# Prompt attention two iterations deep, its second top-k moved, and the gate tiles redistributed, in a two-layer hybrid encoder step

## The reference, cut to what matters

```python
def token_mixing(h, pos, past, w_in, b_forget, w_branch, w_out):
    qkv_sb, qkv_fox, f_logit, qkv_dsa, q_idx, k_idx, w_idx, gate_logit = jnp.split(h @ w_in, offs, axis=-1)
    ...
    o_sb = stick_breaking_attention(q_sb, ks_sb, vs_sb, pos, k_pos)
    o_fox = forgetting_attention(q_fox, ks_fox, vs_fox, g_all[:, -t:], g_all, pos, k_pos)
    o_dsa = dsa_attention(q_dsa, ks_dsa, vs_dsa, q_idx, w_idx, ks_idx, pos, k_pos)
    y = jnp.stack([o.reshape(b, t, MIX_W) for o in (o_sb, o_fox, o_dsa)], axis=2)
    y = jnp.einsum('btnc,ncd->btnd', y, w_branch)
    gates = jax.nn.sigmoid(gate_logit.reshape(b, t, N_BRANCH, D_MODEL))
    merged = jnp.sum(gates * y, axis=2)
```

## Time and profile before

| | |
|---|---|
| median of 3 runs | 2898.83 us (2898.41 to 2899.73) |
| the profiled execution | 2894.99 us, span 2893.2 us |
| TensorE matmul busy | 2642.7 us, 91% of the span |
| VectorE, ScalarE busy | 663.9 us (23%), 514.9 us (18%) |
| DMA moved | 389.01 MB, mean 134 GB/s |
| granted TensorE clock, mean | 0.962 |

### The profile page before, as it was taken

How to read it: one execution, slowest core, us unless ns; L and a number is a source line. 1 busy time by engine, 2 the same in 40 slices (tenths; PEclk the granted TensorE clock), 3 DMA queues, 4 the chain that set the end, 5 groups by cost and what they waited for, 6 DMA issues and landing times.

```text
span 2893.2 us, 32024 instructions
## 1 busy us (share of the span) xinstructions
PE 2642.7 (91%) x12900; PEld 1597.7 (55%) x12900; DVE 663.9 (23%) x1452; ACT 514.9 (18%) x1010; POOL 0.2 (0%) x4
## 2 busy tenths in 40 slices
PE   5999998997798899999969999999878979899997
PEld 3666554555565555555546665555555655455554
DVE  2111002024475421110021110100254754211101
ACT  2000002013443311000110000110235332300001
POOL 0000000000000000000000000000000000000000
PEclk8999999998999899999989999999999999999998
DMA  8555332351168531323275543324403694223231
GB/s 301 175 174 192 121 101 66 109 150 57 62 207 265 180 117 58 116 87 100 85 267 185 193 165 109 104 70 116 141 33 121 189 285 147 88 88 107 87 100 62
DMA packets 315597, 389.01 MB, mean 134 GB/s; under 512 B 33566, under 2 KB 269850, under 8 KB 315491
## 3 DMA queue, kind: packets, MB, share of 16 engines
q1 hardware_dynamic: 308418, 378.65, 39.6%
q10 hardware_dynamic: 7072, 8.87, 0.9%
HBM read 377.85 MB, written 9.62 MB: 134 GB/s over the span
## 4 chain that ended last, share of the span: by engine, by line
PE 85%; DMA 4%; ACT 4%; DVE 3%; SPq 2%; issue 1%; ACTq 0%; DVEq 0%
PE PS L556 29%; PE PS L597 16%; PE PS L631 11%; PE PS L653 8%; PE PS L843 3%; PE PS L853 3%; PE PS L576 3%; PE PS L534 2%; PE PS L800 2%; PE PS L770 2%; DMA RING<-w_ada 1%; DMA QKT<-cache_dsa_k 1%; PE PS L711 1%; PE PS L522 1%; PE PS L810 1%
## 5 line engine op out<-in xcount | busy, mean ns | idle before, releaser
L556 PE MATMUL PS<-H,RING 128*128 128x384 f32 x2560 | 843.0, 491 | 20.4 <-ACT H L914 20.4
L556 PEld LDWEIGHTS PS<-H,RING 128*128 128x128 f32 x2560 | 488.5, 192 | 360.9 <-issue 33.4
L597 PE MATMUL PS<-BIG,RING 128*128 128x384 f32 x1408 | 458.5, 489 | 9.3 <-DVE BIG L1226 9.3
L597 PEld LDWEIGHTS PS<-BIG,RING 128*128 128x128 f32 x1408 | 269.3, 191 | 198.2 <-issue 14.8
L631 PE MATMUL PS<-RING,H 128*128 128x384 f32 (+1 forms) x960 | 309.2, 486 | 6.8 <-ACT H L914 6.8
L653 PE MATMUL PS<-H,RING 128*128 128x384 f32 x768 | 257.5, 492 | 0.0
L631 PEld LDWEIGHTS PS<-RING,H 128*128 128x128 f32 x960 | 184.0, 192 | 132.2 <-issue 10.4
L1225 DVE TENSOR_TENSOR QR<-PS,QR 128x384 f32<-128x384 f32 x88 | 49.0, 557 | 838.3 <-ACT QR L922 838.3
L922 ACT ACTIVATE QR<-PS 128x384 f32<-128x384 f32 x88 | 43.1, 490 | 908.4 <-PE PS L556 825.3
L653 PEld LDWEIGHTS PS<-H,RING 128*128 128x128 f32 x768 | 145.1, 192 | 97.4 <-issue 6.0
L1181 DVE TENSOR_TENSOR QR<-QR,MOD 128x128 f32<-128x128 f32 x48 | 14.0, 292 | 537.9 <-ACT QR L931 537.9
(11 more groups left out here) (186 smaller groups left out, 1746.5 us busy)
## 6 DMA issues: line engine op xcount, KB each, us to landing
RING<-ffn_w_in SPq DMA_DIRECT2D x88, 1024.0 KB, 7.0
RING<-w_in SPq DMA_DIRECT2D x68, 768.0 KB, 6.1
QR<-w_ada SPq DMA_DIRECT2D x48, 1024.0 KB, 7.1
RING<-w_ada SPq DMA_DIRECT2D x24, 1024.0 KB, 7.4
RING<-ffn_w_out SPq DMA_DIRECT2D x32, 768.0 KB, 4.6
RING<-ffn_w_out SPq DMA_DIRECT2D x32, 640.0 KB, 5.7
QKT<-cache_sb_k SPq DMA_DIRECT2D x16, 768.0 KB, 6.8
QR<-cache_sb_v SPq DMA_DIRECT2D x16, 768.0 KB, 4.5
```

Of the source, the lines that this page charges most:

```text
L556: mm = pe.matmul(PS[:, 2 * jj + part, 0:T], w[:, k, part * 256 + jj * P:part * 256 + (jj + 1) * P], H[:, k, :], start=(k == 0), stop=(k == ...
L597: mm = pe.matmul(PS[:, m, 0:T], w[:, k, m * P:(m + 1) * P], HID[:, half * (NFF // 2) + k, :], start=(half == 0 and k == 0), stop=(half == ...
```

## The change

- **Prompt attention two deep.** `ZP` gets two buffers of two halves each, the softmax statistics two sets. TensorE issues the scores of `it + 2` between the transposes and the values of `it`. VectorE's loop is cut into `biased` (scale, bias, mask), `maxima` and `probs`, and runs `biased(it + 1)`, `probs(it)`, `maxima(it + 1)`; ScalarE runs `exponentials(it + 1)` between the copies of `it` and its output copy. A new semaphore `z_taken` says that the scores' PSUM banks are read. Sigmoids, the SB product and the maxima are made in two halves of three heads.
- **Top-k moved.** The first half's eight rounds go in pairs ahead of the four sample heads' sums in the index stage, the second half's eight into the prompt iterations 0, 2 and 3 (2, 3 and 3 rounds). Both keep their work arrays in `RSTD` and `VAR`.
- **Gate tiles.** None stands between the samples' index heads. Tiles 6 and 7 come after the last one, 8 to 12 at the ends of prompt iterations 0 to 4, 13 to 23 in sample steps 0, 1, 2, 4, 6, 8, 10, 12, 14, 16 and 18. All of 6 to 12 use PSUM bank 4, all of the steps' bank 3.
- **Sample steps.** The samples' 17 top-k rounds go to steps 0 to 8 and 10 (2, 2, 2, 1, 2, 1, 2, 1, 2, 2). The last two gate weight units load after `load_step(2)` and `load_step(7)`; the mask is stored after `load_step(12)` instead of 10.

```diff
-GATES = [6, 8, 9]
-GATE_AT = [9, 10, 11, 12, 13, 14, 15]
-GATE_STEP = {s: GATE_AT[6] + s for s in range(9)}
-ROUND_STEP = {s: 2 for s in range(8)}
+GATES = 6
+GATE_PROMPT = [GATES + 1 + it for it in range(6)]
+GATE_STEP = dict(zip((0, 1, 2, 4, 6, 8, 10, 12, 14, 16, 18), range(13, 24)))
+ROUND_P = {0: 2, 2: 3, 3: 3}
+ROUND_S = {0: 2, 1: 2, 2: 2, 3: 1, 4: 2, 5: 1, 6: 2, 7: 1, 8: 2, 10: 2}
...
-                    if s in (0, 3):
-                        gates(6 + s // 3)
-                    if s == NB + 2:
+                    if s in (2, 7):
+                        gates(6 + s // 7)
+                    if s == NB + 4:
                         sp.wait_ge(msk_ready, l * 3 + 3)
...
-                    if h in (1, 2):
-
-                        pe.wait_ge(relu_ready, l * 6 + 1)
-                        for n in range(GATES[h - 1], GATES[h]):
-                            gate_tile(n, n % 2)
+                    if h == 2:
+                        prompt_scores(0)
+
+                pe.wait_ge(relu_ready, l * 6 + 5)
+                gate_tile(GATES, 4)
+                prompt_scores(1)
+                gate_tile(GATE_PROMPT[0], 4)
                 pe.wait_ge(relu_ready, l * 6 + 6)
...
+                    if it + 2 < 6:
+                        prompt_scores(it + 2)
...
                     mm.then_inc(po_ready, 1)
+                    if it + 1 < 6:
+                        gate_tile(GATE_PROMPT[it + 1], 4)
...
+                take_gate(GATES, 4)
+                exponentials(0)
+                for it in range(6):
+                    r = it // 2
+                    take_gate(GATE_PROMPT[it], 4)
                     for g in range(3):
                         act.wait_ge(pt_ready, l * 18 + (3 * it + g + 1))
...
+                    if it + 1 < 6:
+                        exponentials(it + 1)
...
                 for h in range(IH):
+                    choose(0, 2)
                     dve.wait_ge(relu_ready, l * 6 + (3 + h))
...
+                begin()
+                biased(0)
+                for it in range(6):
+                    begin()
+                    if it + 1 < 6:
+                        biased(it + 1)
+                    probs(it)
+                    if it + 1 < 6:
+                        maxima(it + 1)
+                    if it in ROUND_P:
+                        choose(1, ROUND_P[it])
+                    if it == 3:
+                        mask(1)
...
-                    if s in ROUND_STEP:
-                        choose_some(2 * s, ROUND_STEP[s])
-                    if s == NB:
-                        choose_some(2 * NB, 1)
+                    if s in ROUND_S:
+                        choose_some(sum(n for i, n in ROUND_S.items() if i < s), ROUND_S[s])
+                    if s == max(ROUND_S):
```

More of the change, by code:

```diff
@@ L169, in program @@
         assert o <= 6912
-        ZP, EP, LP = (qr(i * 1536, 1536).rearrange("p (h k) -> p h k", h=NH) for i in range(3))
+        EP, LP = (qr(i * 1536, 1536).rearrange("p (h k) -> p h k", h=NH) for i in (1, 2))
+        ZP = [[qr(o, 768).rearrange("p (h k) -> p h k", h=NPAIR) for o in zs] for zs in ((0, 768), (6144, QX + 1536))]
         PTP = qr(3 * 1536, 1536).rearrange("p (h k q) -> p h k q", h=NH, k=2)
@@ L648, in gate_tile @@
                         full(l, u)
-                    if n >= 2 and bank < 4:
-                        pe.wait_ge(gate_taken, l * 24 + n - 1)
+                    if n >= 2:
+                        pe.wait_ge(gate_taken, l * 24 + n - (1 if n < GATES else 0))
                     w = ring(u % 2, KD, MIX)
@@ L655, in gate_tile @@
                     mm.then_inc(gate_ready, 1)
-                for n in range(GATES[0]):
+                for n in range(GATES):
                     gate_tile(n, n % 2)
@@ L702, in _, with prompt_scores @@
                     mm.then_inc(is_ready, 1)
+                def prompt_scores(it):
+                    r, qt = it // 2, it % 2
+                    if it:
+                        pe.wait_ge(z_taken, l * 6 + it)
+                    for h in range(NH):
+                        s = slice(64 * (h % 2), 64 * (h % 2) + 64)
+                        mm = pe.matmul(PS[:, 2 * (h % 2) + h // 4, (h // 2 % 2) * 256:(h // 2 % 2) * 256 + 256],
+                                       QKT[s, r, 0, h // 2, qt * P:(qt + 1) * P], QKT[s, r, 1, h // 2, :],
+                                       start=True, stop=True)
+                    mm.then_inc(s_ready, 1)
                 pe.wait_ge(it_free, l * 8 + 10)
@@ L1043, in _, with exponentials @@
                           ACT.Relu, scale=1 / 16).then_inc(relu_ready, 1)
[L1044 to L1048, removed]
+                def exponentials(it):
                     r = it // 2
+                    z = ZP[it % 2]
+                    p = 24 * (it % 2)
                     begin()
@@ L1251, in reverse_scan, with choose @@
                 return V.tensor_tensor_scan(out[:, ::-1], terms[:, ::-1], more[:, ::-1], 0.0, ALU.add, ALU.add)
-            def choose(keys, rounds):
-                w = WK[:, 0:keys]
+            def choose(qt, rounds):
                 for _ in range(rounds):
-                    link(V.max(M8, w))
-                    link(V.match_replace(w, M8, w, TAKEN))
+                    link(V.max(M8, WK[qt]))
+                    link(V.match_replace(WK[qt], M8, WK[qt], TAKEN))
             for l in range(DEPTH):
@@ L1337, in _, with biased @@
                     dve.sem_inc(relu_free, 1)
+                mask(0)
                 dve.wait_ge(kidx_stored, l * 32 + 32)
                 dve.sem_inc(is_done, 1)
-                for it in range(6):
+                def biased(it):
                     r, qt = it // 2, it % 2
-                    begin()
+                    Z = ZP[it % 2]
                     dve.wait_ge(s_ready, l * 6 + (it + 1))
@@ L1351, in _ @@
                         bias = GB[:, z::2, :] if r == FOX else bias[:, None, :].to_broadcast([P, NPAIR, NPROMPT])
-                        link(V.scalar_tensor_tensor(out=ZP[:, z * NPAIR:(z + 1) * NPAIR, :], in0=S, scalar=SCALE, in1=bias,
-                                                    op0=ALU.mult, op1=ALU.add))
+                        link(V.scalar_tensor_tensor(out=Z[z], in0=S, scalar=SCALE, in1=bias, op0=ALU.mult, op1=ALU.add))
+                    dve.sem_inc(z_taken, 1)
                     if r == FOX:
-                        link(V.tensor_tensor(ZP, ZP, MASKS[:, 1, qt, :][:, None, :].to_broadcast([P, NH, NPROMPT]), ALU.add))
+                        for z in range(2):
+                            link(V.tensor_tensor(Z[z], Z[z], MASKS[:, 1, qt, :][:, None, :].to_broadcast([P, NPAIR, NPROMPT]), ALU.add))
@@ new lines, in probs @@
+                def probs(it):
+                    Z = ZP[it % 2]
+                    p = 24 * (it % 2)
+                    dve.wait_ge(e_ready, l * 6 + (it + 1))
+                    if it // 2 == SB:
+                        for h in range(NH):
+                            z = Z[h // NPAIR][:, h % NPAIR, :]
+                            link(reverse_product(z[:, 0:NPROMPT - 1], LP[:, h, 1:NPROMPT], ZERO[:, 1:NPROMPT]))
+                        for z in range(2):
+                            e = EP[:, z * NPAIR:(z + 1) * NPAIR, 0:NPROMPT - 1]
+                            ins = V.tensor_tensor(e, e, Z[z][:, :, 0:NPROMPT - 1], ALU.mult)
+                            if z == 0:
+                                link(ins)
+                    else:
+                        link(V.reciprocal(ST[:, p + 16:p + 16 + NH], ST[:, p + 8:p + 8 + NH]))
+                        ins = V.tensor_tensor(EP, EP, ST[:, p + 16:p + 16 + NH][..., None].to_broadcast([P, NH, NPROMPT]), ALU.mult)
+                    ins.then_inc(p_done, 1)
+                    dve.wait_ge(p_done, l * 6 + (it + 1))
```

78 lines of the change are left out of this document (30 added, 48 removed).

## The result

The changed kernel takes **2905.89 us** (median of 12 runs, 2896.78 to 2920.15), the kernel before 2898.05 (12 runs, 2895.00 to 2902.38): a ratio of **1.0033 [1.0017, 1.0048]**. It is slower by a little, where 2878, 21 us faster, was forecast. The runs of the changed kernel spread over 23 us, those of before over 7. The profiled execution of the changed kernel is the slowest of its 12, 2920.15 us (span 2918.4, mean granted clock 0.949), so its trace shows more of the loss than the median holds: 25 us above the profiled execution of before, not 8.

The account below looks back on a forecast made before the run. TensorE was taken as the bound in steps 0 to 9, idle in waits in prompt attention and steps 10 to 19. Layers gave -11.2 and -9.6, together -20.8: 2894.99 to 2874.2, plus 3.84, forecast 2878, range 2861 to 2893.

Parts of the forecast that it names:

- The first transposes: Layer 0 prompt attention: TensorE can transpose the first probabilities at 710.4.
- Prompt iterations 2 to 4: Prompt attention: TensorE sets the pace, 10.1 us per iteration from iteration 1, and 9.5 for the one without scores.
- Pairs of early steps: Sample steps 0 to 9: a gated and an ungated step take 9.45 + 4.3 + 1.8 = 15.6 us.
- The loop that binds steps 10 to 19: Values end, value load, bias loads, key load, landing, key turn, gate tile, values; one loop is two steps.
- 16.9, say 17.0 a pair: Steps 10 to 19: load loop per two steps, 85 us for five, 18.4 us more than before in layer 0.
- I take 4.9, near the lower end: Steps 10 to 19: key load's landing time in us, between 4.4 and 6.45, since DMA would be less full.
- The estimate of 3.8 us by that fit: Key load's landing by 2.0 us plus bytes over 436 GB/s, 11 us less over both layers; not used.
- rival (c): Steps 10 to 19: clock falls in the pairs' waits, turn, tile and values cost 6.8 us more per pair, 2946; chance 0.06.
- The prompt attention: Layer 0 up to the first key turn: ends at 768.7 against 790.5, 21.8 us less.
- Steps 0 to 9: Sample steps 0 to 9: 87.3 us, 7.8 us less than 95.1.
- The wait at step 8: Step 8's key load lies behind gate weights and FOX bias loads on SP's queue: 2.5 us, bounds 0 and 5.
- forecast -11.2: Layer 0 sum in us: -21.8 prompt attention, -7.8 steps 0 to 9, +18.4 steps 10 to 19.

Follow-up runs that it names:

- experiments 1 and 5: 1: changed kernel with values ahead of the gate tile in sample steps, 2867.09 us; 5: changed kernel with key loads issued one load_step earlier, 2849.61 us.
- Experiment 6: Changed kernel with values ahead of the gate tile, plus the prompt's first sigmoids ahead of the copy of gate tile 6: 2862.30 us.
- experiment 4: Changed kernel plus five matmuls into an unused result ahead of the key turn in gated steps 8 to 18: 2892.65 us.
- experiment 2: Changed kernel with its eleven sample gate tiles in steps 0 to 10 and top-k rounds in steps 0 to 8: 2880.86 us.

## Why the prediction was wrong

**Where it held.** The first transposes came at 708.7 in a frame 2.1 earlier than before's (forecast 710.4). Prompt iterations 2 to 4 took 10.1, 10.1 and 9.5 us, as forecast. Pairs of early steps took 15.7 us (15.6), with the waits for the output rows' copy in them. The loop that binds steps 10 to 19 is link for link the one named, from values to key load 3.9 us; experiments 1 and 5 show that cutting it at either of two places takes most of the tiles' price away.

**The step that failed** is the price of that loop: "16.9, say 17.0 a pair". Over the five gated pairs of layer 0 the chain has landings of 5.87, 5.40, 6.76, 5.84 and 5.12, mean 5.8, where "I take 4.9, near the lower end"; turns of 2.64 on average where 1.53 was taken; tiles of 6.46 where 5.17 was. That is 0.9 + 1.1 + 1.3 = 3.3 us a pair, 16.5 for five, and the window is 101.3 against 85 forecast: all of the 16.3 that is missing there. In layer 1 the three terms are 0.3, 0.8 and 0.9, some 10 for five pairs, and its window is 94.5 against 85:

```profile
2308.80:2403.30 94.50, 79.00 (x683) 52.38 (x680) 36.31 (x104) 26.97 (x47) 0.00 (x0) 0.89 0.62 195
```

- *The landing.* The reason given, "with DMA less full than now", read a mean over a stage as if it were the state at the time of the load. Beside the 4.99 of the earlier trace rows the chain of the kernel before has these landings in the same stage of layer 0 (start, us, what):

```profile
889.94 5.93 DMA QKT<-cache_fox_k
...
902.76 5.99 DMA QKT<-cache_fox_k
...
929.08 5.39 DMA QKT<-cache_dsa_k
...
943.14 4.50 DMA QKT<-cache_dsa_k
```

  Their mean is 5.4, and the ten gated pairs of the changed kernel have 5.5: the landings did not get shorter, and 4.9 was too low for either kernel. The share did fall, to 0.59, but the loads come in a bunch: SyncE's queue of the changed kernel, right after the key load of 880.54, shows a value load 0.9 us later and the next keys 6 us later.

```profile
880.54 0.63 SPq L432 DMA_DIRECT2D QKT<-cache_fox_k  x1
881.46 0.39 SPq L462 DMA_DIRECT2D QR<-cache_fox_v  x1
...
886.67 0.44 SPq L432 DMA_DIRECT2D QKT<-cache_fox_k  x1
```

  That the value load is what slows the keys was not tried by itself. The Trainium skill (DMA: Bandwidth & Descriptors, Anatomy of one DMA) gives its fit for the path of GpSimd, while SyncE issues these loads. The estimate of 3.8 us by that fit was met nowhere in these pairs; 4.45 is the shortest.
- *The clock.* This is rival (c), which got 0.06 because "each pair now holds 14 us of matmuls around one wait". That was no protection. Of the ten gated turns of steps 10 to 18 over both layers, seven take 2.82 us, two 1.81 and 1.93, one 1.53. But (c)'s price was off as well: it let turn, tile and values all run at the lower clock, 6.8 us a pair. The tile loses 1.3 instead of 4.3 and the values run at their full-clock 1.38, so the clock is back before the tile ends, and the price in layer 0 is 2.4. The Trainium skill (TensorE: Matmul & The Clock Gate, HAM oscillation) tells of a kernel with short matmul bursts that loses the clock at every wait for a DMA; the trace agrees for nine of the ten turns, though these pairs hold longer bursts.

**The prompt attention** gave 17.7 us instead of 21.8. Of the missing 4.1, 0.4 are the later first transposes, and the rest is the clock again: 2.6 in iteration 0 (16.2 against 13.6, where both the transposes and the scores run at the lower level after the wait of 4.92) and 1.1 in iteration 1 (11.2 against 10.1), whose transposes take 2.92. I had costed them at the durations of the earlier trace rows, which follow a wait of 2.32. Experiment 6 shows it from the other side: with a wait of 1.85 iteration 0 takes 13.9.

**Steps 0 to 9** took 91.0 instead of 87.3. The wait at step 8 was inside its bounds in layer 0 (4.76 against 2.5 with bounds of 0 and 5) and outside in layer 1 (5.75); the turn and the tile after it ran at a lower clock, which was not costed.

In sum, layer 0: forecast -11.2; the four misses are 4.1, 3.7, 16.3 and 0.1, together 24.2, and the profiled execution is at +13.0 (994.1 less 983.2, and the 2.1 that it started earlier). Layer 1 missed by as much: -9.6 forecast, +12.8 measured, with 16.5 us won in the prompt attention, 2.9 in steps 0 to 9, 29.5 lost in steps 10 to 19 and 2.7 in the rest. The profiled execution is the slowest of the runs. The median is 14 us lower, and experiment 4, which holds the clock in the gated pairs, lies another 13 below that. Over the 12 runs the mean granted clock goes with the time, from 0.957 in the fastest (2896.78) to 0.949 in the slowest; as an estimate from these two, 0.008 of 2900 us is 23 us of full-clock work, the width of the spread. Which pairs keep the clock in the faster runs is not shown, since only one execution was profiled.

## What to carry to other kernels

Before filler work goes into an engine's idle time, ask what the instructions behind the filler release: here the tile delayed values, values a value load, and the next key load stood behind that load on one in-order queue. Issue the load that bounds a loop ahead of any load that has to wait, and the filler costs less than half its length instead of more than all of it (12 and 35 us for 26 us of tiles; 2905.9 to 2849.6 us with three lines changed). When a new wait is costed, cost the work behind it at the lower clock too, until it is seen at the higher one.

## What the runs showed of the hardware

- The same length of wait does not decide the clock by itself. In experiment 2, same layer, two turns follow waits of 2.23 and 2.11 us; the first turn keeps the clock, the second, after the shorter wait, does not:

```profile
890.78 1.53 PE L770 MATMUL PS<-IDENT,QKT 128*128 128x128 f32 x12 [2.23 <-DMA QKT<-cache_fox_k]
...
897.44 2.82 PE L770 MATMUL PS<-IDENT,QKT 128*128 128x128 f32 x12 [2.11 <-DMA QKT<-cache_fox_k]
```

- Useless matmuls can pay: 39 us of them over both layers (12 times 3.25) made the kernel 13 us faster in experiment 4, since they ran where TensorE was idle anyway and kept its clock.
- A stage's DMA share says little of a single load. On the chain of layer 0, key loads of the same 768 KB landed in 5.1 to 6.8 us in a stage with a share of 0.59, and in 4.5 to 6.0 us in one with 0.93.
